# A mixture-of-experts layer on one core: weights in a ring of four thirds, TensorE's code written out per ring position, and list rows taken earlier on VectorE

## The chip, the core and the metric

The kernel runs on one core of a Trainium2 chip. Its engines are TensorE (PE in the rows; PEld is its weight load), VectorE (DVE), ScalarE (ACT), GpSimd (POOL) and SyncE (SP, which here issues the weight transfers). The metric is the device time of one execution in microseconds.

## What is computed

One layer on 1024 tokens of width 1024. A mixer comes first (a gated linear recurrence and a spatial gating unit between two projections, with adaptive norms); the part of this study is the mixture of experts behind it, 32 experts, four for each token:

```python
logits = hf @ router_w + router_b
top_logit, top_e = lax.top_k(logits, 4); gates = softmax(top_logit)
# for each block of rows of one expert e:
gu = xb @ w_gu[e] + b_gu[e]                 # 1024 -> 2048, f32
g, lin = split(gu); g = min(g, 7); lin = clip(lin, -7, 7)
ys = (g * sigmoid(1.702 * g) * (lin + 1)) @ w_down[e] + b_down[e]
out[row_tok] += ys * row_gate               # then residual, rmsnorm
```

All weights are f32: 8 MB of `w_gu` and 4 MB of `w_down` for each expert.

## The kernel before

The mixer and the router take the first 480 us or so. Then the tokens of each expert are cut into units of 32 rows, and up to four units form an item, which all engines handle in one pass of a loop. The router's result makes a table of items in SBUF (`items_i`): for each item its expert, first row, number of units, units before it, and its expert's place in the order. The places alternate between experts with many and with few tokens, and the last ones are alike. How many units an item has is read into registers at run time; `by_units` branches over the code for units that are not there. Here there are 32 places, 47 items and 143 units.

An expert's weights come in 12 chunks of 1 MB, numbered q, in three thirds of four: chunks 0 to 3 are the rows k 0 to 3 of the gate and linear weights, 4 to 7 the rows k 4 to 7, and 8 to 11 the down weights. They lie in `big`, six slots of 16 KB in each partition, and each third has its fixed two slots (`gu_slab`, `down_slab`, `chunk_tile`). SyncE's queue loads place after place. Before a third it waits until TensorE has released that third in the last item of the place before:

```python
if q % 4 == 0:
    sp_.wait_ge(freed[q // 4], done)
load_chunk(e, q)
```

`freed[0]` rises with the first matmul of the second half of the gate and linear product, `freed[1]` with the first matmul behind that half (a list's), `freed[2]` with the first matmul behind the down product. TensorE waits for each chunk with `w_arrived[q]` in the first unit of an item.

TensorE's loop, for item g: `down_of(g)` makes the list of item g+5 (`make_list`, L1159), multiplies the units by the down weights (L1226) and repeats the list's rows over partitions (`repeat_rows`, L1171); then `gate_and_linear_of(g + 1)` multiplies the next item's rows by the gate and linear weights (L1206), first half k 0 to 3 for all units, then the second. So the loop's back edge stands between a gate product and the down product of the same item.

VectorE's pass for item g: turn the gathered rows of item g+1 (`block_rows`, L1818), make the one-hot table of g+3 (L1810), the activations of g's units (L1858 to L1873), take the repeated list rows of g+4 and make indices and gates of g+2 (L1679 to L1695), read list g+5 (L1674), and write the results (L1878, L1881). GpSimd gathers the rows of g+2 when their indices are there, and then scatters the results of g into `acc_rows`. ScalarE scales the turned rows (`z_made`) and does the sigmoids.

The tile `r1` (32 KB in each partition) holds the hidden rows until they have been written out before the experts, and again at the end for the last norm.

## Time and profile before

| | |
|---|---|
| median of three executions | 2146.21 us (2138.85 to 4163.29) |
| the profiled execution | 2144.11 us, span 2142.4 us |
| mean granted TensorE clock | 0.968 |
| TensorE, VectorE, GpSimd, ScalarE busy | 91%, 47%, 24%, 17% |
| moved by DMA | 527 MB, 246 GB/s over the span |
| experts' part, first to last gate or down matmul | about 480 to 2111.6 us |

A row of the timeline merges equal instructions; in brackets stands the engine's idle time before them and who ended it. Busy shares of TensorE count its matmuls at whatever clock it had.

### The profile page before, as it was taken

Reading aid. Unit: us, or ns where it says so; the run is one execution under the profiler, and the core shown is the slowest. Engines: PE = TensorE matmul, PEld = TensorE weight load, DVE = VectorE, ACT = ScalarE, POOL = GpSimd, SP = SyncE. Lnnn points to the kernel's source line nnn. Section 1 sums busy time; section 2 is a strip of 40 time slices with the busy share of each in tenths; the row PEclk is TensorE's granted clock in tenths of the full one; section 3 lists DMA queues with packets and bytes.
Section 4 is the critical chain, followed back from the end, with each engine's and each line's share of the span. In section 5 each row is a group of like instructions: output and inputs, shape, how many; then the busy total and the mean of one; then the engine's idle time right before and its main releaser. Section 6 shows DMA issues by size and latency. Waiting matters only on the chain.

```text
span 2142.4 us, 53085 instructions
## 1 busy us (share of the span) xinstructions
PE 1960.0 (91%) x20253; PEld 803.5 (38%) x20254; DVE 1004.2 (47%) x2276; ACT 355.7 (17%) x729; POOL 508.6 (24%) x536
## 2 busy tenths in 40 slices
PE   3998999978989989999999998999999999999994
PEld 2443444432424323433343342334333343334332
DVE  6427756345434434444444454444443544444434
ACT  3025311221011111111111111111111111011012
POOL 3000022121312322313131322233233322322322
PEclk9998999988989989999999999999999999999997
DMA  9332126322581773959496969879797897999985
GB/s 330 128 118 78 63 95 196 138 109 97 197 340 29 237 300 95 353 177 355 161 352 224 355 251 367 301 266 391 256 387 252 296 357 266 386 385 338 325 305 187
DMA packets 128956, 527.19 MB, mean 246 GB/s; under 512 B 17184, under 2 KB 47920, under 8 KB 79760
## 3 DMA queue, kind: packets, MB, share of 16 engines
q1 hardware_dynamic: 95344, 470.39, 56.6%
q0 software_dynamic: 33568, 56.29, 11.4%
q8 instruction: 19, 0.31, 0.1%
q14 instruction: 25, 0.20, 0.0%
HBM read 494.22 MB, written 32.38 MB: 246 GB/s over the span
## 4 chain that ended last, share of the span: by engine, by line
PE 74%; DMA 14%; DVE 5%; SPq 3%; ACT 2%; issue 1%; POOL 1%; DVEq 0%; POOLq 0%; ACTq 0%
PE psum L1206 39%; PE psum L1226 21%; DMA big<-in_exp_w_down_dram 6%; DMA big<-in_exp_w_gu_dram 6%; PE psum L1115 5%; PE psum L959 5%; PE psum L1052 2%; SPq L466 1%; DMA big<-in_w_in_dram 1%; PE psum L999 1%; DVE big L1453 1%; SPq L447 0%; PE psum L1159 0%; DVE r L1926 0%; DVE gacc L1391 0%
## 5 line engine op out<-in xcount | busy, mean ns | idle before, releaser
L1206 PE MATMUL psum<-big,r 128*32 128x512 f32 x9152 | 1017.5, 602 | 53.8 <-DMA big<-in_exp_w_gu_dram 42.6
L1206 PEld LDWEIGHTS psum<-big,r 128*32 128x32 f32 x9152 | 290.3, 111 | 732.5 <-issue 653.8
L1226 PE MATMUL psum<-big,r 128*32 128x256 f32 x9152 | 518.3, 385 | 27.3 <-DMA big<-in_exp_w_down_dram 16.4
L1226 PEld LDWEIGHTS psum<-big,r 128*32 128x32 f32 x9152 | 294.1, 111 | 230.1 <-DMA big<-in_exp_w_down_dram 26.3
L859 ACT ACTIVATE r<-r,shift 128x128 f32<-128x128 f32 x376 | 154.2, 480 | 998.8 <-PE psum L1206 941.7
L666 POOL DMA_INDIRECT acc_rows<-r,scatter_idx x143 | 230.8, 1614 | 84.9 <-POOL scatter_idx L697 42.9
L655 POOL COPY gather_idx<-r 128x4 int32 (+1 forms) x48 | 8.9, 186 | 1017.5 <-DVE r L1688 1017.5
L1858 DVE TENSOR_TENSOR r<-psum,r 128x256 f32<-128x256 f32 x143 | 60.6, 424 | 377.7 <-PE psum L1206 376.8
L658 POOL DMA_INDIRECT r<-hs_rows,gather_idx x192 | 192.3, 1002 | 85.3 <-issue 45.4
L1818 DVE STREAM_TRANSPOSE r<-r 128x1024 f32<-128x1024 f32 x47 | 97.9, 2084 | 175.8 <-DMA r<-hs_rows,gather_idx 112.6
L959 PE MATMUL psum<-r,big 128*128 128x512 f32 x384 | 167.8, 598 | 2.8 <-DMA big<-in_w_in_dram 2.8
L1878 DVE TENSOR_TENSOR r<-psum,r 128x256 f32<-128x256 f32 x143 | 60.8, 425 | 227.8 <-PE psum L1226 214.0
L866 ACT ACTIVATE r<-r 128x256 f32<-128x256 f32 x143 | 59.5, 416 | 393.6 <-DVE r L1864 393.6
L1115 PE MATMUL psum<-big,r 128*128 128x512 f32 x256 | 112.2, 595 | 0.6 <-DMA big<-in_w_out_dram 0.4
L959 PEld LDWEIGHTS psum<-r,big 128*128 128x128 f32 x384 | 73.4, 192 | 94.1 <-issue 91.1
L1873 DVE STREAM_TRANSPOSE r<-r 128x256 f32<-128x256 f32 x143 | 93.5, 654 | 4.9
L1869 DVE TENSOR_TENSOR r<-r 128x256 f32<-128x256 f32 x143 | 60.8, 425 | 50.3 <-ACT r L866 50.3
L1881 DVE SCALAR_TENSOR_TENSOR r<-r,g1row,g_rows 128x256 f32<-128x256 f32 x143 | 69.3, 485 | 5.1
L1115 PEld LDWEIGHTS psum<-big,r 128*128 128x128 f32 x256 | 47.9, 190 | 59.0 <-issue 57.7
L1391 DVE SCALAR_TENSOR_TENSOR gacc<-big,cact,gacc 128x512 f32<-128x512 f32 x84 | 63.2, 752 | 3.0
L608 POOL TENSOR_TENSOR r<-r,big 128x512 f32<-128x512 f32 x8 | 12.0, 1496 | 216.6 <-DVE r L1545 216.6
L1871 DVE TENSOR_TENSOR r<-r 128x256 f32<-128x256 f32 x143 | 60.8, 425 | 4.9
(284 smaller groups left out, 975.1 us busy)
## 6 DMA issues: line engine op xcount, KB each, us to landing
big<-in_exp_w_gu_dram SPq DMA_DIRECT2D x256, 1024.0 KB, 10.5
big<-in_exp_w_down_dram SPq DMA_DIRECT2D x128, 1024.0 KB, 14.0
big<-in_ada_w_dram SPq DMA_DIRECT2D x12, 2048.0 KB, 12.8
r<-in_x_dram SPq DMA_DIRECT2D x16, 512.0 KB, 12.5
big<-in_w_in_dram SPq DMA_DIRECT2D x4, 2048.0 KB, 20.3
r<-in_exp_b_gu_dram SPq DMA_DIRECT2D x128, 64.0 KB
big<-in_w_out_dram SPq DMA_DIRECT2D x2, 2048.0 KB, 13.3
hs_rows<-r POOLq DMA_DIRECT2D x8, 512.0 KB, 2.9
```

The source lines that it names most:

```text
L658: pool.indirect_dma_start(z_quarters[:, u, :], None, hs_quarters, bass.IndirectOffsetOnAxis(ap=gather_idx[:, u:u + 1], axis=0)).then_inc(r ...
L666: pool.indirect_dma_start(acc_quarters, bass.IndirectOffsetOnAxis(ap=scatter_idx[:, u:u + 1], axis=0), y_sb[:, u, :], None, bounds_check=4 ...
L859: ins_ = act.activation(izT[:, k, :].rearrange("p (u n) -> p u n", u=UMAX), z_blocks[:, :, k, :], ACT.Identity, bias=shift2[:, 1, k:k + 1] ...
L959: last = pe.matmul(b, w[:, k, m * P:(m + 1) * P], zT[:, k, th * 512:(th + 1) * 512], start=(k == 0), stop=(k == KT - 1))
L1115: last = pe.matmul(b, src[:, ct % CT, t * P:(t + 1) * P], ring(("wout", dh))[:, ct, :], start=(ct == 0), stop=(ct == 2 * CT - 1))
L1206: last = pe.matmul(psum[32 * j:32 * j + 32, u, :].rearrange("p (a n) -> p a n", a=2), izT[:, k, u * UNIT:(u + 1) * UNIT], rhs[:, :, 256 * ...
L1226: ins_ = pe.matmul(psum[32 * i:32 * i + 32, 4 + u % 2, 0:256], actT[:, u, f, :], down_slab(f)[:, 256 * i:256 * i + 256], start=(f == 0), s ...
L1391: ins_ = dve.scalar_tensor_tensor(out=a, in0=w[:, k, :], scalar=cact[:, k:k + 1], in1=a, op0=ALU.mult, op1=ALU.add)
L1818: dve.transpose(z_blocks, z_quarters.rearrange("p u (n k) -> p u k n", k=KT)).then_inc(z_blocked, 1)
L1869: dve.tensor_tensor(gsig_sb[:, u % 2, :], gate_u, sig_sb[:, u % 2, :], ALU.mult).then_inc(gsig_made, 1)
L1873: dve.transpose(actT[:, u, :, :], act_sb[:, u % 2, :].rearrange("p (n k) -> p k n", k=KT)).then_inc(at_made, 1)
L1881: dve.scalar_tensor_tensor(out=y_sb[:, u, :], in0=y_sb[:, u, :], scalar=gate_cur[:, u:u + 1], in1=g2_rows[:, :], op0=ALU.mult, op1=ALU.mul ...
```

## The change

There are four thirds in the ring: the three in `big`, and `r1` as the fourth. Third c of place p lies in ring third (3p + c) mod 4, so the position of an expert's weights repeats every four places. A third is loaded when the third four loads before it has been released: that is the down third of place p-2 for c = 0, and the two gate thirds of place p-1 for c = 1 and 2. The semaphores of arrival exist twice, for even and odd places.

Since TensorE's addresses are fixed in its code, its body is written once for each of the four positions. Place 0 has its own code, places 1 to 28 go through an outer loop of seven trips over four bodies, and places 29 to 31 have three more. Each body is a loop over the items of its place, with ends read from the table. Within an item the gate and linear product now comes first and the down product second, which is the same sequence of products as before with the loop's edge elsewhere.

On VectorE, `rows_here`, `make_idx` and `make_gates` move from behind the activations to the place behind `block_rows`.

```diff
@@ SyncE and the tiles
-        w_arrived = [sem(f"w_arrived{q}") for q in range(CHUNKS)]
+        w_arrived = [[sem(f"w_arrived{q}_{turn}") for q in range(CHUNKS)] for turn in range(2)]
+        def third_of(place, c):
+            return (3 * place + c) % THIRDS
+        def in_third(third, at, size):
+            if third == THIRDS - 1:
+                return r1[:, at:at + size]
+            return big[:, SLOT_OF_PAIR[2 * third + at // 4096], at % 4096:at % 4096 + size]
-        def gu_slab(k):
-            at = (k % 2) * 2048
-            return big[:, SLOT_OF_PAIR[k // 2], at:at + 2048]
+        def gu_slab(place, k):
+            return in_third(third_of(place, k // 4), (k % 4) * 2048, 2048)
...
             for place in range(1, NE):
-                done = sp_.value_load(items_i[0:1, CUM_ITEMS + place - 1:CUM_ITEMS + place], min_val=1, max_val=MAX_ITEMS)
+                done_before, done = done, items_until(place - 1)
                 for q in range(CHUNKS):
-                    if q % 4 == 0:
-                        sp_.wait_ge(freed[q // 4], done)
-                    load_chunk(e, q)
+                    if q == 0 and place >= 2:
+                        sp_.wait_ge(freed[2], done_before)
+                    if q == 4:
+                        sp_.wait_ge(freed[0], done)
+                    if q == 8:
+                        sp_.wait_ge(freed[1], done)
+                    load_chunk(place, e, q)
@@ TensorE
             def begin_item():
-                pe.reg_alu(place, loaded[0], 0, ALU.max)
-                pe.reg_alu(units, loaded[1], 1, ALU.max)
-                pe.reg_alu(before_, loaded[2], 0, ALU.max)
-                pe.reg_mul(arrived, place, SEMW)
-                pe.reg_add(arrived, arrived, SEMW)
+                pe.reg_alu(units, loaded[0], 1, ALU.max)
+                pe.reg_alu(before_, loaded[1], 0, ALU.max)
+            def begin_place(at):
+                if at % 2 == 0:
+                    pe.reg_add(arrived, arrived, SEMW)
+                pe.reg_alu(first_item, next_item, 1, ALU.max)
+                pe.reg_alu(next_item, loaded[2], 1, ALU.max)
...
-            with pe.Fori(0, last_item) as g:
-                down_of(g)
-                begin_item()
-                gate_and_linear_of(g + 1)
-            down_of(last_item)
+            def items_of(at, start, place):
+                with pe.Fori(start, next_item) as g:
+                    begin_item()
+                    gate_and_linear_of(at, g, place)
+                    down_of(at, g)
+            down_of(0, 0)
+            by_units(pe, next_item, 1, lambda: items_of(0, 1, 0))
+            with pe.Fori(0, (NE - 4) // THIRDS) as i:
+                for at in range(1, THIRDS + 1):
+                    begin_place(at)
+                    items_of(at, first_item, i * THIRDS + at)
+            for place in range(NE - 3, NE):
+                begin_place(place)
+                items_of(place, first_item, place)
@@ VectorE
                 block_rows(g + 1)
+                rows_here(g + 4, step)
+                make_idx(g + 2, step)
+                make_gates(g + 2, step)
                 make_onehot(g + 3)
...
                 by_units(dve, units, 1, activate_1)
-                rows_here(g + 4, step)
-                make_idx(g + 2, step)
-                make_gates(g + 2, step)
                 read_list(g + 5)
```

TensorE, between the last down product of one item and the next gate product. Before (L1171 repeats the list's rows, L1188 sets the item's registers, L1206 is the first unit's gate product; no branch stands between them):

```order
L1171 MATMUL psum<-g1row,r2 128x6 x4
L1188 ISA
L1206 MATMUL psum<-big,r2 32x512 x16
L395 COMPARE_AND_BRANCH
L395 UNCONDITIONAL_BRANCH
```

Now, at the end of the first of the four bodies (L1249 is the down product, L1187 the repeat, L1380 the loop over a place's items, L1213 the next place's registers, L1229 the gate product of the next body):

```order
L1249 MATMUL psum<-big,r2 32x256 x32
L398 UNCONDITIONAL_BRANCH x3
L1187 MATMUL psum<-g1row,r2 128x6 x4
L1380 REGISTER_ALU
L1380 COMPARE_AND_BRANCH
L1213 ISA
L1380 UNCONDITIONAL_BRANCH
L1380 ISA
L1229 MATMUL psum<-big,r2 32x512 x16
L396 COMPARE_AND_BRANCH
L396 UNCONDITIONAL_BRANCH
```

The back edge has moved to this place, and a place's registers are set behind it. The outer loop holds four such bodies one behind the other, where the loop before held one.

SyncE's queue, the second third of a place (place 2 before, place 2 now), behind the bias rows of that place. Before:

```order
L473 ISA
L473 DMA r2<-in_exp_b_gu_dram 32x2x256
L476 ISA
L476 DMA r2<-in_exp_b_down_dram 32x256
L466 ISA [waits freed1]
L466 DMA big<-in_exp_w_gu_dram 128x2048
```

Now:

```order
L480 ISA
L480 DMA r2<-in_exp_b_gu_dram 32x2x256
L483 ISA
L483 DMA r2<-in_exp_b_down_dram 32x256
L473 ISA [waits freed0]
L473 DMA r1<-in_exp_w_gu_dram 128x2048
```

The wait is for the release of the first third instead of the second, and this load goes to `r1`.

VectorE, the head of the loop's pass, from the transpose of gathered rows on. Before, the one-hot table (L1800, L1810) follows it:

```order
L1818 STREAM_TRANSPOSE r<-r 128x1024 [waits z_made1,z_made0,rows_in]
L388 ISA
L388 TENSOR_LOAD r
L388 ISA x3
L388 TENSOR_LOAD r
L388 ISA x2
L1800 ISA
L1800 COPY g1row<-r 128x48
L1810 ISA
L1810 REGISTER_ALU
L1810 TENSOR_TENSOR r<-r 128x1024
```

Now the list rows and the indices stand there (L1720 to L1729), and the one-hot table behind them:

```order
L1859 STREAM_TRANSPOSE r<-r 128x1024 [waits z_made1,z_made0,rows_in]
L1719 REGISTER_ALU
L1720 COPY g1row<-psum 128x24 [waits rows_repeated]
L1886 ISA
L1725 SCALAR_TENSOR_TENSOR g1row<-g1row 128x4 [waits dve_chain]
L1886 REGISTER_ALU
L1727 SCALAR_TENSOR_TENSOR g1row<-g1row,slot_quarter 128x4 [waits dve_chain]
L1886 REGISTER_ALU
L1729 ISA [waits dve_chain]
L1729 SCALAR_TENSOR_TENSOR r<-g1row,quarter 128x4
L1735 TENSOR_TENSOR g1row<-g1row 128x4
```

Six small operations have moved ahead of the one-hot table, with a wait for the repeated rows in front of them.

## Rows read from the trace of the kernel before

**Rows 1.** The page's sections 1 and 2: busy share, and 40 slices of the span.
```profile
PE 1960.0 (91%) x20253; PEld 803.5 (38%) x20254; DVE 1004.2 (47%) x2276; ACT 355.7 (17%) x729; POOL 508.6 (24%) x536
...
GB/s 330 128 118 78 63 95 196 138 109 97 197 340 29 237 300 95 353 177 355 161 352 224 355 251 367 301 266 391 256 387 252 296 357 266 386 385 338 325 305 187
```

**Rows 2.** TensorE's waits from 546.5 us.
```profile
PE psum L1206 <- DMA big<-in_exp_w_gu_dram: 42.6, 25, 2.8
PE psum L1226 <- DMA big<-in_exp_w_down_dram: 16.4, 16, 1.5
PE psum L1226 <- DVE r L1873: 6.2, 2, 3.1
```

**Rows 3.** The chain of waits, 1827 to 1902 us: start us, us, what.
```profile
1827.87 20.74 PE psum L1206 x192
...
1859.58 27.60 PE psum L1206 x256
1887.18 0.29 PE psum L1159 x8
...
1901.60 0.55 PE psum L1206
```

**Rows 4.** Windows: us, busy us (x count) of PE, PEld, DVE, ACT, POOL; clock, DMA, GB/s.
```profile
546.50:588.50 42.00, 42.00 (x528) 16.85 (x525) 18.73 (x47) 4.86 (x12) 10.77 (x11) 1.00 0.68 235
605.80:2111.60 1505.80, 1444.80 (x17680) 565.48 (x17680) 673.45 (x1688) 196.02 (x486) 407.11 (x399) 0.98 0.78 285
1849.00:2111.00 262.00, 262.00 (x3332) 107.19 (x3328) 117.72 (x301) 31.07 (x77) 69.29 (x67) 1.00 0.87 318
...
40.00:480.00 440.00, 398.98 (x1310) 190.06 (x1310) 231.46 (x348) 116.43 (x145) 46.11 (x51) 0.96 0.35 123
```

**Rows 5.** SyncE's queue, 1566 to 1589 us: start us, us, issues merged.
```profile
1566.20 1.89 SPq L466 DMA_DIRECT2D big<-in_exp_w_gu_dram  x4
...
1575.76 1.92 SPq L466 DMA_DIRECT2D big<-in_exp_w_gu_dram  x4
1586.55 1.88 SPq L466 DMA_DIRECT2D big<-in_exp_w_down_dram  x4
```

**Rows 6.** DMA engines from 1626 to 1659 us: queue, packets, MB, share.
```profile
q1 hardware_dynamic: 2017, 11.41, 88.9%
```

**Rows 7.** TensorE's timeline, passes of one unit (751) and two (1586).
```profile
751.19 4.13 PE L1226 MATMUL psum<-big,r 128*32 128x256 f32 x48 [3.09 <-DVE r L1873]
...
1586.20 0.25 PE L1171 MATMUL psum<-g1row,r 128*128 128x6 bf16 x4
1586.38 9.65 PE L1206 MATMUL psum<-big,r 128*32 128x512 f32 x88
1596.57 4.50 PE L1206 MATMUL psum<-big,r 128*32 128x512 f32 x40 [0.54 <-DMA big<-in_exp_w_gu_dram]
```

**Rows 8.** VectorE by line, 606 to 2111 us; its timeline at 748 and 1671.
```profile
L1818 DVE STREAM_TRANSPOSE r<-r 128x1024 f32<-128x1024 f32 x44 | 91.7, 2084 | 168.1 <-DMA r<-hs_rows,gather_idx 112.6 <-issue 55.4
...
748.07 0.42 DVE L1858 TENSOR_TENSOR r<-psum,r 128x256 f32<-128x256 f32 x1 [0.86 <-PE psum L1206]
...
1670.47 0.13 DVE L1679 COPY g1row<-psum 128x24 f32<-128x24 f32 x1
...
1671.74 0.16 DVE L1695 TENSOR_TENSOR r<-g1row 128x4 f32 x1
```

**Rows 9.** DMA queues: 40 to 480, 500 to 606, and two in 606 to 2095.
```profile
q8 instruction: 11, 0.18, 0.2%
...
q8 instruction: 6, 0.10, 0.4%
...
q0 software_dynamic: 27295, 40.19, 12.9%
q14 instruction: 16, 0.13, 0.0%
```

**Rows 10.** The chain's last transfer but one.
```profile
2114.68 3.66 DMA acc_rows<-r,scatter_idx
```

100 lines of the change are left out of this document (55 added, 45 removed).

## The prediction

> **What bounds the kernel now.** I read the page's busy shares first: TensorE is busy 91% of the span [rows 1], and no other engine reaches 50%. The experts' part therefore hangs on TensorE, and the question is what it loses there. The waits of TensorE from 546.5 us on have only three entries: 42.6 us for chunks of the gate and linear weights, 16.4 us for chunks of the down weights, 6.2 us in two waits for VectorE's turned activations [rows 2]. Nothing else holds it.
>
> Then the price of an undisturbed pass. With no wait a pass of four units takes 27.60 us for gate and linear, 0.29 for a list and 14.13 for the down product and the rows' repeat, 42.0 in all, and one of three units 31.7 (from 1827.87 to 1859.58) [rows 3]; so a unit costs 10.4 us (6.9 gate and linear, 3.5 down) and a pass 0.45 on top. Counting the matmuls of each pass in the timeline, the stretch from 605.8 us to the last matmul at 2111.6 has 44 passes: 15 of four units, 17 of three, 11 of two and one of one unit. Undisturbed that is 15 x 42.0 + 17 x 31.7 + 11 x 21.4 + 11.0 = 1415 us. (That is 134 units: at 128 matmuls a unit and 12 a pass they make the 17,680 of the window's row, [rows 4].) It took 1505.8 us, so 90.5 us are lost: 61.0 idle (it was busy 1444.8), and 29.5 in which TensorE ran, but partly at the lower of its clock's two levels: the stretch has a mean granted clock of 0.98, the undisturbed end from 1849 on 1.00 and no idle time [rows 4]. Of the 90.5, 6.5 belong to the pass of one unit near 751 us, whose down product waits for its own activations [rows 7]: no weight is late there. **84 us hang on late weights**, waits and the slower clock behind them.
>
> Why they are late: the queue that loads weights waits until the third of the ring that it refills is released, and the release is in the same expert's last pass. In rows 5 the loads of one expert go out at 1566.20, 1575.76 and 1586.55 us, the moments at which the previous expert (its pass began 31.7 us before 1586.38, at 1554.7, [rows 7]) lets go of its thirds. Over the stretch behind them the DMA engines are nearly full: the weights' queue has 88.9% of their time and brings 11.41 MB in 33 us [rows 6]. So a chunk of 1.05 MB takes 3.0 us as it stands, 2.7 if the queue had all their time, and an expert's twelve 32 to 36 us, but a pass of three units lasts 31.7 and one of two 21.4. So after short passes TensorE meets chunks that have not landed: 0.54 us and then more in the pass that begins at 1586.38 [rows 7], 59.0 us in all.
>
> **The ring of four thirds.** Third c of place p now replaces the third used four loads earlier: its first third waits for the down product of place p-2, its second for the first half of p-1, its last for the second half of p-1. Everything may start one third earlier, 10 to 15 us. For the expert of rows 5: its first third could go at 1554.8 instead of 1566.2, the second at 1566.2 instead of 1575.8, the last at 1575.8; behind each other at 2.9 us a chunk they end near 1567, 1579 and 1591, and the down product wants the last only at 1601 [rows 5, 7]. The stall is gone with 8 us to spare.
> I stepped through all passes in this way (units from the instruction counts, four chunks per third, each 2.85 to 2.95 us and 2.3 us more until landing, no load before its third is released). With the releases of before it gives 57 to 78 us of waits where the trace has 59.0 [rows 2], and at the same passes; with the releases of the change 3 to 7 us, nearly all in two passes that follow very short experts. With the lower clock behind them I leave 7 us: **84 - 7 = 77 us gained**. Place 1 loads its first third already when the item table is ready, near 500 us, into the tile that held the hidden rows; the DMA engines are nearly idle there (the slices near 500 us have 97 and 197 GB/s, [rows 1]), so I take nothing for it.
>
> **VectorE's order.** The list rows of item g+4 and the indices of g+2 are made ahead of the activations instead of behind them. Its transpose of gathered rows waited 112.6 us for gathers [rows 8], but TensorE has no wait for gathered rows in this stretch [rows 2], so the earlier gather gains nothing on the path. What moves ahead is six small operations, from 1670.47 to 1671.90: 1.5 us. What is queued behind them is the one-hot table and the first activation, for which TensorE waits in turn. Even in the pass of one unit VectorE sat idle 0.86 us before that activation, until the gate product was there [rows 8]; a unit more gives 6.9 us more. So only two passes, of one unit each, lose 0.6 us: **1 us lost**.
>
> **TensorE's program.** Before, one body served all passes. A pass of four units executes 256 + 256 + 12 matmuls (256 and 8 of them in [rows 3]) and as many weight loads, with some 40 register and branch instructions about 1,090. Now four such bodies stand in a row inside the outer loop, three more behind it. What code costs to bring in shows only before: eleven code packets of 16 KB (0.18 MB) on queue 8 fall between 40 and 480 us, in which 1,310 matmuls and 1,310 loads ran, so with the waits between them a packet holds about 256 instructions and a body is 4.2 of them; and from 606 to 2095 us queue 8 has none [rows 4, 9]. So a body once fetched stays, across 45 back edges. And while the first trip brought its body in, with six packets between 500 and 606 us, the gate product from 546.5 ran at full speed: 42.0 us busy of 42.0 [rows 4, 9]. Straight code is therefore hidden. Four bodies are 17 packets; the trace shows at least five held at once, and does not show seventeen. If those do not stay, the inner loops (14 back edges in places with several items) still find their own body, but the outer loop's back edge, taken six times, finds its first block gone, and nothing can be fetched ahead of a jump back by 17 blocks. The price of one such miss no row has. From below it is nothing; from above I take the nearest transfers that nothing overlaps, above all the last scatter's 3.66 us [rows 10], with as much again for a second block and the slower clock: 0 to 8 us. TensorE's queue covers little, since the matmuls of the down product leave it fastest. I take 3.5 us, near that row: **6 x 3.5 = 21 us lost** (0 to 48).
> The rows say that code of 4.2 blocks is kept through 45 jumps back. The Trainium skill, "Runtime: NRT & Kernel Launch", section "Instruction fetch mechanics", has both sides: TensorE's instruction memory is 128 KiB, eight blocks of 16, which this agrees with; and a taken branch whose target is outside a window of two pages stalls for a fetch, which it does not, since each back edge of before goes back four blocks and no packet follows. By the eight blocks the sum stays as it is.
> The new words on a place (one compare, a few register operations and a load more) stand where the last down product is still queued; the boundary of before has no idle time between the repeat and the next product (1586.20 + 0.25, then 1586.38, [rows 7]), and I take zero, 0.3 us x 31 = 9 at most.
>
> **Sum**, against the profiled execution's own 2144.1 us (span 2142.4 and 1.7 around it; 2.1 below the median of the runs shown, 2146.2): 2144.1 - 77 + 1 + 21 = 2089, so **2090 us**, 2.6% below.
>
> **Rivals.** *Code is also missed at forward jumps.* A pass with fewer than four units jumps over up to three branches of its body, and counted along the built program with the units of each pass, 37 such jumps in first visits cross a block's end. No row of before shows a jump into code not yet fetched (its first trip had all four units), so this can be. If the block after the target is then late, 2.2 us each time: 37 x 2.2 = 81 us on top, 2171 us, slower than before; it turns slower than before from 1.5 us a jump. Against it: a block ahead was always there in the first trip. The skill's window of two pages, on the page named above, would also act here and at the 14 inner back edges.
> *Nothing is missed*: the outer loop's code stays or is fetched behind the queue. 2144.1 - 77 + 1 = 2068.
> *The thirds come no sooner in effect*: loads that start earlier meet the scatter and gather packets (12.9% of the DMA engines' time [rows 9]) and the chunks take 3.3 us; then the walk leaves some 20 us of waits and 12 of slow clock, 25 more than I took, with the code's part 2115; were only half the waits to go, 2128.
>
> **How the numbers follow.** The forecast has 0.55 (2072 to 2112), nothing missed 0.15 (2068), the jumps 0.18 (2120 to 2195), late chunks 0.12 (2110 to 2135). The range 2063 to 2140 leaves out most of the jumps' case. A measurement of this kernel tells about 2% from no change: faster means below 2103, slower above 2189. Faster: nearly all of the first two, 0.67; same 0.26; slower 0.07, from the jumps' case with 3 us and more each.
>
> **What would show it.** Waits of TensorE for the weights' DMA under 10 us in all, a mean clock of 1.00 from 800 us on, the weights' queue waiting on the repeat of the list rows. Code packets on queue 8 going on through the experts' part, some 130; a gap of TensorE with no releaser at every fourth place (six of them), and none in passes with a jump. VectorE's wait for gathers well under 112 us. I am wrong if those gaps come at every place, if they are longer than 8 us, or if the weights' waits stay above 30 us.

## The result and the profile after

The changed kernel takes 2195.2 us (median of four, 2191.7 to 2197.1), the kernel before in the same comparison 2144.4: a ratio of 1.024, 95% interval 1.022 to 1.027. Two later comparisons gave 1.023 and 1.022. It is slower by 51 us where 2.6% faster was forecast; 2195 lies outside the range.

The profiled execution took 2196.3 us, span 2194.6, 52 more than before. TensorE's waits from 546.5 us (us in total, times, longest), which answer to [rows 2]:

```profile
PE psum L1229 <- issue: 39.6, 25, 6.3
PE psum L1187 <- issue: 38.9, 15, 5.4
PE psum L1249 <- issue: 8.8, 7, 1.6
PE psum L1175 <- DVE r L1851: 5.9, 2, 2.9
PE psum L1249 <- DVE r L1917: 5.3, 2, 2.6
```

The weights have left the list altogether: not one wait for a chunk is left of 59.0 us. In their place stand 47 waits "<- issue", 87.3 us, idle time for which the profile shows no releaser, at the gate product (L1229), the repeat (L1187) and the down product (L1249). The windows that answer to [rows 4] (us, busy us (x count) of PE, PEld, DVE, ACT, POOL, then clock, DMA share, GB/s):

```profile
546.50:588.50 42.00, 42.00 (x532) 16.84 (x528) 18.93 (x48) 4.85 (x12) 11.87 (x11) 1.00 0.62 221
605.80:2163.80 1558.00, 1464.77 (x17724) 596.37 (x17720) 683.03 (x1690) 196.09 (x486) 433.65 (x398) 0.97 0.78 275
1901.00:2163.80 262.80, 261.64 (x3324) 108.53 (x3317) 117.73 (x294) 31.08 (x77) 70.70 (x62) 1.00 0.83 292
615.20:2163.80 1548.60, 1460.83 (x17664) 594.55 (x17668) 680.18 (x1688) 196.09 (x486) 432.01 (x397) 0.97 0.78 275
```

From 605.8 us to the last matmul the experts' stretch is 1558.0 us instead of 1505.8. The changed kernel is already 9.4 us behind at its start: it has the rest of a pass of one unit in there, with a gap of 5.0 us behind it. The 44 passes of before begin only at 615.2 (last row) and take 1548.6 us, 42.8 more: idle is 87.8 instead of 61.0, and the other 16 us are matmuls at the lower clock (1460.8 busy instead of 1444.8). The last passes, of four units each, are undisturbed as before. The page's DMA queues:

```profile
q1 hardware_dynamic: 95344, 470.39, 56.1%
q0 software_dynamic: 33568, 56.29, 11.6%
q8 instruction: 163, 2.67, 0.5%
q14 instruction: 25, 0.20, 0.0%
```

Queue 8, which carries code, alone from 606 to 2095 us, where before it moved nothing [rows 9]:

```profile
q8 instruction: 135, 2.21, 0.6%
```

So the code packets are there that the prediction gave as "some 130". Where the gaps are shows in TensorE's timeline: first a pass of one unit, which answers to the first of [rows 7], then the outer loop's back edge and the pass of two units behind it, and one of the later back edges (start us, us; in brackets the idle time before):

```profile
744.17 7.07 PE L1229 MATMUL psum<-big,r 128*32 128x512 f32 x64
754.18 0.37 PE L1175 MATMUL psum<-g1row,r 128*128 128x6 bf16 x8 [2.93 <-DVE r L1851]
757.19 5.51 PE L1249 MATMUL psum<-r 128*32 128x256 f32 x64 [2.64 <-DVE r L1917]
767.52 0.24 PE L1187 MATMUL psum<-g1row,r 128*128 128x6 bf16 x4 [4.82 <-issue]
768.24 10.25 PE L1229 MATMUL psum<-big,r 128*32 128x512 f32 x80 [0.47 <-issue]
...
874.96 0.25 PE L1187 MATMUL psum<-g1row,r 128*128 128x6 bf16 x4
877.88 2.77 PE L1229 MATMUL psum<-r 128*32 128x512 f32 x21 [2.66 <-issue]
883.36 6.61 PE L1229 MATMUL psum<-r 128*32 128x512 f32 x42 [2.71 <-issue]
...
897.48 7.11 PE L1249 MATMUL psum<-big,r 128*32 128x256 f32 x128
908.89 0.25 PE L1187 MATMUL psum<-g1row,r 128*128 128x6 bf16 x4 [4.30 <-issue]
...
1502.62 13.86 PE L1229 MATMUL psum<-r 128*32 128x512 f32 x95 [6.32 <-issue]
```

These gaps end with code. From 546.5 us on 25 gaps without a releaser are longer than 0.8 us, and each of them ends 2.4 to 3.0 us after a packet of queue 8 begins (worked out from the packets' start times).

There are two kinds of gap. One stands at each of the six outer back edges (877.88, 1110.14, 1316.31, 1502.62, 1690.87, 1876.09), ahead of the first body's gate product: 33.3 us idle in all, 3.9 to 6.3 each. Behind the one at 1502.62 the granted clock is 0.79, and 95 matmuls take 13.9 us that elsewhere take 10.3. The other, 54 us, stands mostly behind short down products on a first visit to a body: in front of the repeat at 767.52 and 908.89. First visits of four units have at most 0.5 us ahead of their gate product, and the same holds for a place's second item in the same body.

Per pass, from one gate product's start to the next (mean us of two profiles of each kernel; a first visit is a place's first item; worked out from the matmuls' start times, without place 0; the undisturbed pass of one unit is an estimate from the others, 10.3 us a unit):

```
units  visit  passes  undisturbed  before  changed
1      first     2        11.1      17.3    23.9
2      first    11        21.4      25.7    27.0
3      first     9        31.7      34.2    33.9
3      later     8        31.7      31.7    34.9
4      first     9        42.0      43.8    42.6
4      later     6        42.0      42.0    43.0
```

The later visits of three and four units that grow are those in front of an outer back edge. Of the eleven first visits of two units three stand behind one and take 32 to 34 us; the other eight average 24.9 (22.3 to 27.0). On VectorE the transpose no longer waits for gathers (before 112.6 us, [rows 8]):

```profile
L1859 DVE STREAM_TRANSPOSE r<-r 128x1024 f32<-128x1024 f32 x47 | 97.0, 2064 | 116.3 <-issue 111.2 <-DMA r<-hs_rows,gather_idx 5.1
```

### The profile page after: what moved, and what is told of

Same layout as the page of the kernel before. It is cut to its first block, busy times and chain, and to the rows that moved or that the text cites. A ratio compares the mean times of both kernels' runs of the same rounds, so it can differ in the third digit from the quotient of the medians.

```text
span 2194.6 us, 53308 instructions
## 1 busy us (share of the span) xinstructions
PE 1976.3 (90%) x20253; PEld 833.1 (38%) x20254; DVE 1013.7 (46%) x2276; ACT 356.0 (16%) x729; POOL 535.3 (24%) x536
## 4 chain that ended last, share of the span: by engine, by line
PE 83%; issue 5%; DVE 5%; DMA 2%; ACT 2%; SPq 1%; DVEq 1%; POOL 1%; ACTq 0%; POOLq 0%
PE psum L1229 46%; PE psum L1249 23%; PE psum L1131 5%; PE psum L975 4%; PE psum L1068 2%; DMA big<-in_w_in_dram 1%; PE psum L1015 1%; PE psum L1175 1%; DVE big L1494 1%; SPq L454 0%; DVE r L1967 0%; SPq L463 0%; DVE gacc L1432 0%; PE psum L1187 0%; DVE big L1510 0%
## 5 line engine op out<-in xcount | busy, mean ns | idle before, releaser
L1229 PE MATMUL psum<-big,r 128*32 128x512 f32 x6912 | 780.5, 606 | 17.7 <-issue 9.8
L1249 PE MATMUL psum<-big,r 128*32 128x256 f32 x7744 | 431.1, 381 | 12.4 <-issue 5.9
L1229 PEld LDWEIGHTS psum<-big,r 128*32 128x32 f32 x6912 | 238.6, 112 | 516.0 <-issue 506.3
L1249 PEld LDWEIGHTS psum<-big,r 128*32 128x32 f32 x7744 | 248.6, 110 | 177.2 <-issue 11.0
L1229 PE MATMUL psum<-r 128*32 128x512 f32 x2240 | 265.0, 618 | 33.3 <-issue 33.3
L674 POOL DMA_INDIRECT r<-hs_rows,gather_idx x192 | 222.9, 1161 | 87.8 <-issue 45.7
L1229 PEld LDWEIGHTS psum<-r 128*32 128x32 f32 x2240 | 81.3, 113 | 205.5 <-issue 205.4
L1249 PE MATMUL psum<-r 128*32 128x256 f32 x1408 | 80.9, 386 | 5.5 <-issue 2.9
L1913 DVE TENSOR_TENSOR r<-r 128x256 f32<-128x256 f32 x143 | 60.9, 426 | 50.1 <-ACT r L882 50.1
## 6 DMA issues: line engine op xcount, KB each, us to landing
big<-in_exp_w_gu_dram SPq DMA_DIRECT2D x192, 1024.0 KB, 10.6
```

The source lines that it names most:

```text
L674: pool.indirect_dma_start(z_quarters[:, u, :], None, hs_quarters, bass.IndirectOffsetOnAxis(ap=gather_idx[:, u:u + 1], axis=0)).then_inc(r ...
L1229: last = pe.matmul(psum[32 * j:32 * j + 32, u, :].rearrange("p (a n) -> p a n", a=2), izT[:, k, u * UNIT:(u + 1) * UNIT], rhs[:, :, 256 * ...
L1249: ins_ = pe.matmul(psum[32 * i:32 * i + 32, 4 + u % 2, 0:256], actT[:, u, f, :], down_slab(at, f)[:, 256 * i:256 * i + 256], start=(f == 0 ...
L1913: dve.tensor_tensor(gsig_sb[:, u % 2, :], gate_u, sig_sb[:, u % 2, :], ALU.mult).then_inc(gsig_made, 1)
```

## The experiments

Theory A, formed from this trace: TensorE's code arrives one block of 256 instructions at a time, the next is asked for only when the one before is entered, and comes about 5.9 us later; a body has 4.2 blocks whatever its units, so a first visit lasts some 25 us, and at an outer back edge nothing is there at all. Rival B is the one on record, a price of some 2.2 us for each jump over a block's end. Others: VectorE's move, and the ring itself (the tile `r1`, more DMA at a time). In two of the five comparisons that follow the kernel before took 2218 us (beside VectorE's move, the bodies alone, the loop written out and three jumped blocks) and 2193 us (beside the repeated move and the two forms with two bodies), in the others 2143 to 2146. The end of this section comes back to that; the kernels of those two are read by their own medians and traces. Each of the five ran on a chip of its own, so differences between kernels of different comparisons rest on their times being the same on those chips: the change took 2191.5 and 2191.9 us on two of them, and VectorE's move alone 2158.1 and 2158.5 on the two others.

**VectorE's move alone.**

```diff
                 block_rows(g + 1)
+                rows_here(g + 4, step)
+                make_idx(g + 2, step)
+                make_gates(g + 2, step)
                 make_onehot(g + 3)
...
-                rows_here(g + 4, step)
-                make_idx(g + 2, step)
-                make_gates(g + 2, step)
```

> The kernel before with VectorE's move alone (list rows, indices and gates ahead of the one-hot table and the activations). Three theories of the 51 us by which the change lost. Theory A (TensorE's code arrives too slowly for short passes and is missed at the outer back edge) and theory B (code missed at each jump over a block's end) both put nothing here: 2144 to 2150 us, with 1.5 us more in front of the one-hot table of a pass of one unit and VectorE's wait for gathers down from 112 us to under 20. Theory C, the move delays what TensorE waits for: 2165 us and more.

2158.1 us; span 2157.7. Against the kernel before of its own comparison that is a ratio of 0.973, against the medians of before elsewhere, 2144, it is 14 us more, between what theories A and B gave (2144 to 2150) and what C gave (2165 and more). The waits of TensorE from 546.5 us:

```profile
PE psum L1206 <- DMA big<-in_exp_w_gu_dram: 41.7, 28, 2.9
PE psum L1226 <- DMA big<-in_exp_w_down_dram: 17.8, 16, 2.0
PE psum L1159 <- DVE r L1810: 5.9, 2, 3.0
PE psum L1226 <- DVE r L1876: 5.3, 2, 2.7
```

The weights' waits are those of before (59.5 us), and in the two passes of one unit the one-hot table is now late as well. It was repeated later:

> The kernel before with VectorE's move alone, once more: in its first comparison the kernel before took 2218 us on that chip, which no profile explains, and on two others 2144. If the move costs what the two profiles show (2157.7 against 2142.4 and 2142.9 us), the ratio is 1.007 (2155 to 2162); if that chip alone made it so, 1.000 to 1.002.

2158.5 us, span 2156.9; the kernel before 2192.7 this time, ratio 0.984 (0.982 to 0.986). The move alone costs some 14 us against a kernel before of 2144, and not 1. Five of them are seen as waits; the rest lies in passes of three and four units that follow short ones and in the clock, and I haven't traced it further.

**The change without it**: the same three lines put back.

> The changed kernel with VectorE's order as before; all else stays. With the move alone the profiled span was 2157.7 us against 2142.4 and 2142.9 of two profiles of the kernel before, of which the two passes of one unit explain 3 us, where I had forecast 1 us in all. If the move costs the same inside the change, this gives 2175 to 2180 us; if it only costs where nothing else is late, 2187 to 2192.

2187.9 us, ratio 1.019 (1.017 to 1.021) against 1.022 and 1.023 of the whole change. Inside the change the move costs about 4 us by the medians of the same level (2191.5 and 2191.9) and 6 to 8 by those two ratios, whose intervals overlap with this one. So it is a small part of the loss of 46 to 51 us, some 4 to 8 us of it.

**The four bodies with a ring of three.**

```diff
         def third_of(place, c):
-            return (3 * place + c) % THIRDS
+            return c
...
-                    if q == 0 and place >= 2:
-                        sp_.wait_ge(freed[2], done_before)
-                    if q == 4:
-                        sp_.wait_ge(freed[0], done)
-                    if q == 8:
-                        sp_.wait_ge(freed[1], done)
+                    if q % 4 == 0:
+                        sp_.wait_ge(freed[q // 4], done)
```

> The changed kernel's TensorE program (four bodies in the outer loop, item loops, parity semaphores) and VectorE order, but all bodies read the same three thirds, and the loads wait for their releases as before: the ring of four is taken out. Theories A and B: the code's idle time stays (about 80 us of gaps without releaser) and the waits for weights come back, less than the 59 us of before because short passes are now longer: 2215 to 2265 us. Theory C, the ring itself or its releases cost the time (more DMA contention, the tile that held the hidden rows): back to 2144 to 2155.

2209.5 us, just under the range. Its waits:

```profile
PE psum L1225 <- issue: 39.7, 23, 5.8
PE psum L1183 <- issue: 32.3, 10, 6.2
PE psum L1225 <- DMA big<-in_exp_w_gu_dram: 16.9, 13, 2.1
...
PE psum L1245 <- issue: 5.4, 4, 2.7
PE psum L1245 <- DMA big<-in_exp_w_down_dram: 5.3, 5, 1.4
```

77 us without a releaser, with the old addresses and releases: the gaps come with the four bodies and not with the ring. Of the 59 us of waits for weights only 22.2 return, since the passes that were too short for their weights are now longer than they. What the ring of four saves this program is therefore only 14 to 18 us (2209.5 less 2195.2 to 2191.5, across comparisons). This is where most of the expected gain went: late weights and late code hit the same short passes.

**The outer loop written out**: `for place in range(1, NE)` instead of the outer loop and its three places behind.

> The changed kernel with its outer loop written out: 31 bodies in a straight line, no outer back edge. Theory A: the six gaps at an outer back edge (33 us idle, 5.5 each, and the slower clock behind them) go, the gaps in passes of one, two and three units stay: 2150 to 2162 us, every pass of one or two units on its first visit at 24 to 26 us. Theory B (a price per jump): the same total, but the gaps move with the jumps' places relative to the blocks' ends. If instead the loop's code of 17 blocks was partly kept and used again on later trips, written out it is worse: above 2200.

2158.4 us, 33 to 37 less than the changed kernel in its three comparisons, and 61.3 us "<- issue" instead of 87.3:

```profile
PE psum L1187 <- issue: 39.6, 11, 5.7
PE psum L1229 <- issue: 12.3, 15, 3.5
PE psum L1249 <- issue: 7.8, 7, 2.0
```

The waits of the gate product, where the back edges were, have shrunk; those in front of the repeat (L1187), behind short passes, stay: first visits of two units take 26.8 us on average, as in the change (27.0). So an outer back edge costs 6 us net. At its own place it costs more, some 9 us (the pass in front of it is longer by 3 to 7 us than with the loop written out, the one behind by 2 to 5), and the other passes together are some 15 us shorter; why is not shown.

**One more block in each body, jumped over.** It tells A from B.

```diff
+            def hop(blocks):
...
+                with pe.If_lt(units, UMAX + 1):
+                    pe.nop()
+                with pe.Else():
+                    for _ in range(128 * blocks):
+                        pe.matmul(psum[:, 6, 0:6], onehot[:, 0, :], cur6[:, 0, :], start=True, stop=True,
+                                  skip_group_check=True)
...
                     gate_and_linear_of(at, g, place)
+                    hop(1)
                     down_of(at, g)
```

> The changed kernel with one more block of code in each body, never executed, jumped over between the gate product and the down product. Theory A (blocks come in order, one at a time, about 5.9 us apart, whatever is jumped over): a first visit now lasts at least 5.3 x 5.9 = 31 us, so passes of one and two units grow by 6 to 7 us, those of three by 0 to 2, those of four not at all: 14 short first visits, about 2280 us. Theory B (a price of about 2.2 us for each jump over a block's end): all 31 first visits grow by 2.2 us, those of four units as well: 2260 us. Theory A2 (only the block behind the running one is fetched ahead, so a jump over a whole block finds nothing): a full miss of 5.5 us in each of 31 first visits, 2360 us.

2281.2 us, ratio 1.064 (1.062 to 1.066): 90 us more than the change. Its two largest waits from 546.5 us, and in the timeline two first visits, of three and of two units:

```profile
PE psum L1175 <- issue: 97.5, 26, 7.5
PE psum L1229 <- issue: 38.1, 20, 6.0
```

```profile
1644.57 20.81 PE L1229 MATMUL psum<-big,r 128*32 128x512 f32 x192
1667.73 0.35 PE L1175 MATMUL psum<-g1row,r 128*128 128x6 bf16 x8 [2.35 <-issue]
...
1681.07 14.92 PE L1229 MATMUL psum<-big,r 128*32 128x512 f32 x128
1699.41 0.37 PE L1175 MATMUL psum<-g1row,r 128*128 128x6 bf16 x8 [3.42 <-issue]
```

The mean first visit grew, against the second profile of the change, by 4.9 us with one unit, 4.5 with two, 2.9 with three and 0.2 with four; later visits not at all. Rival B, a price per jump, would give the same to all; a full miss for each jumped block would give 5.5 to all. Neither holds: a jumped block costs only as much as the work in front of it fails to cover. At four units a gate product lasts 27.7 us, and on average nothing is left of it, though single passes of the nine change by 1.9 us down to 2.2 up. That is theory A. Its total, 2280, came out only because two misses met: the short passes grew by 4.5 to 4.9 us instead of 6 to 7, and those of three units by 2.9 instead of 0 to 2, since 5.3 blocks take about as long as their 31.7 us.

How long a block takes isn't a fixed figure. In the change the packets around a pass of two units begin at 875.06, 880.98, 886.90, 893.32, 899.52, 906.19 and 912.32, so 5.9 to 6.7 us apart, with a DMA share of 0.99. In an undisturbed first visit of four units they are up to 14 us apart (1963.31, 1976.83, 1988.43, 1994.76), so the fetch follows the work and doesn't run ahead of it; that it is the entry into a block that asks for the next is inferred from this. Where the engines are nearly idle they can come closer together: the last pass of the kernel with the down third doubled, below, has them at 2055.42, 2059.46 and 2063.37 (DMA share 0.24), with TensorE waiting for the first two. Some come 3 to 4 us apart under a full load as well. No run changed the load alone, so whether the weights' traffic makes code late stays open.

**How much code stays.** Four kernels with the loop of before and more code in it: three and five blocks never executed and jumped over (`hop(3)`, `hop(5)` between the down product and `begin_item`), the whole body written twice and taken in turn, and the same with the second half of the gate product shared.

```diff
+            def by_turn(body):
...
+                with pe.If_lt(turn_, 1):
+                    body()
+                with pe.Else():
+                    body()
...
             with pe.Fori(0, last_item) as g:
-                down_of(g)
-                begin_item()
-                gate_and_linear_of(g + 1)
+
+                def pass_():
+                    down_of(g)
+                    begin_item()
+                    gate_and_linear_of(g + 1)
+
+                by_turn(pass_)
+                pe.reg_alu(turn_, turn_, 1, ALU.bitwise_xor)
```

> The kernel before with three blocks' worth of code (384 matmuls with their loads) that is never executed, jumped over once in each pass between the down product and the next gate product: the body is 7.3 blocks instead of 4.3. If TensorE keeps eight blocks and a jump within kept code is free: 2144 to 2150 us and no code packets in the experts' part after the first trips. If it keeps only about the five blocks that the trace of before shows, each pass finds its first block gone: at least 5.5 us a pass, 2390 us and more.

> The kernel before with five blocks of code that is never executed, jumped over once in each pass: a loop of 9.3 blocks. The loops of 6.3 and 7.3 blocks had no code packet after the first trips. If the limit is the place for eight blocks, counted over all that lies between the first and the last, each pass now fetches its code again: a miss of 5.5 to 6.3 us at the back edge, one more at the hop, and no pass shorter than its blocks arrive; with the five blocks that are executed alone each pass lasts at least 37 us, about 2650 us in all; if the hopped blocks are fetched too, 55 us a pass and 3150 us. If only executed blocks are kept and counted: 2144 to 2225, like the loop of 7.3.

> The kernel before with the body of its item loop written twice (the same weights, the same waits), the passes taking one and the other in turn: 8.6 blocks of code, all of them executed, where the padded loops of 7.3 and 9.3 had 4.3 executed ones. If TensorE keeps eight executed blocks, nothing is kept here: each of 46 passes begins with a jump over or back by more than four blocks, 5.5 us idle and the slower clock behind, and passes of two units last at least 25 us: 2400 to 2460 us, with some 200 code packets. If more is kept (16 would do, and then the 17 blocks of the change just miss it): 2144 to 2155.

> As the loop of two bodies, but with the second half of the gate and linear product shared: 7.5 blocks, all executed. If eight are kept: 2145 to 2155 us, a few code packets more in the first trips and none behind. If the limit is nearer the 6.3 executed blocks that the kernel with two down products kept: as the loop of two bodies, 2350 us and more.

With three jumped blocks 2222.3 us at a kernel before of 2218.2 (ratio 1.002), with five 2147.6 at 2145.7 (1.001, interval 1.000 to 1.002): both cost nothing, and both have 21 code packets in all, where before has 19. The two bodies took 2349.6 and the shared form 2298.4 at a kernel before of 2192.7 (1.071 and 1.048), the first less than the 2400 to 2460 that I expected, the second between its two forecasts. Their code packets from 606 to 2050 us:

```profile
q8 instruction: 212, 3.47, 1.0%
```

```profile
q8 instruction: 149, 2.44, 0.7%
```

Counted by me in the built programs (no trace shows where a block ends), the code in use in a pass or in two touches 6 blocks with the jumped ones (out of 8 and 10 that the loop spans), and 9 and 8 with the two bodies; the kernel with two down products, below, uses 7 and keeps them. So up to 7 blocks in use stay, 8 do not, and blocks that are only jumped over don't count. By size alone, 6.3 blocks in use stay and 7.5 do not. My expectation for 7.5 blocks was wrong: it took blocks by their size and not by the ends they cross. The Trainium skill, "Runtime: NRT & Kernel Launch", section "Instruction fetch mechanics", gives TensorE 128 KiB of instruction memory, refilled in blocks of 16 KiB, so eight blocks. The runs keep at most seven; that the eighth is taken by the block fetched ahead would fit, but none of them shows it. The outer loop of the change, with 17, is far above.

**Better without code: weights released by chunk.** The ring stays three thirds and the body one; only the release changes.

```diff
+                    if k < KT - 1:
+                        last.then_inc(chunk_read[k], 1)
...
                 for q in range(CHUNKS):
-                    if q % 4 == 0:
-                        sp_.wait_ge(freed[q // 4], done)
+                    sp_.wait_ge({KT - 1: gu_made, CHUNKS - 1: dn_made}.get(q, chunk_read[q]), read)
                     load_chunk(e, q)
```

(`read` is the number of units in the places before, from the same table; in the down product `chunk_read[8]` to `[10]` rise in the same way.)

> The kernel before with one body and three thirds, but each weight chunk released by itself: the last matmul that reads chunk q in each unit counts up a semaphore of its own, and the weights' queue waits for as many units as the places before have. The same walk through the passes that gave the forecast has 62 us of waits for weights with releases by thirds (the trace of before has 59) and 30 with releases by chunk. No code is added to TensorE, so theory A expects no gap without releaser: 84 us of cost fall to about 42, 2102 us (2085 to 2120). If the DMA engines are the bound rather than the late release, waits and time stay: 2135 to 2144.

2106.9 us, ratio 0.982 (0.979 to 0.985). The waits for weights fell to 32.3 us, and no wait is without a releaser:

```profile
PE psum L1206 <- DMA big<-in_exp_w_gu_dram: 23.6, 17, 2.5
PE psum L1228 <- DMA big<-in_exp_w_down_dram: 8.7, 8, 1.4
PE psum L1228 <- DVE r L1877: 6.2, 2, 3.1
```

**And with the down weights' third alone doubled** into `r1`, so that only the down product exists twice in the one body:

```diff
+                with pe.If_lt(odd_place, 1):
+                    down_by(0)
+                with pe.Else():
+                    down_by(1)
```

> The kernel before with releases by chunk and with the down product's third alone doubled (odd places read it from the tile that held the hidden rows), so that TensorE's one body has two down products, 6.3 blocks in all instead of 18 in the loop. The walk has 21 us of waits: 84 us fall to about 30, 2090 us (2075 to 2110), if a body of 6.3 blocks stays and runs at full speed. If it behaves as the padded body of 7.3 blocks did (3.2 us in each pass of three and four units), 70 to 100 us are added: 2160 to 2190. If a larger body is fetched again at each back edge, at least 5.5 us in each of 46 passes: 2340 and more.

2109.3 us, ratio 0.983 (0.980 to 0.987): no better than by chunk alone, and at the upper end of the range. The waits for down weights are gone, but the last pass, which stands behind the loop, is new code with a jump over two blocks in it:

```profile
2056.02 0.35 PE L1177 MATMUL psum<-g1row,r 128*128 128x6 bf16 x8
2058.17 1.24 PE L1252 MATMUL psum<-r 128*32 128x256 f32 x17 [1.79 <-issue]
2061.74 15.37 PE L1252 MATMUL psum<-r 128*32 128x256 f32 x239 [2.34 <-issue]
```

The last place is an odd one, so its branch can be dropped (`if last: down_by((NE - 1) % 2)`):

> The kernel with releases by chunk and the down product's third doubled, but the down product of the last item, which stands behind the loop, written for odd places alone (the last place is 31). The trace of that kernel had 6.8 us more in this pass than the kernel before: code that was jumped to two blocks ahead. If those are missed code, 2109 falls to 2103 (2100 to 2105); if they are not, it stays.

2102.6 us, ratio 0.980 (0.978 to 0.982), as forecast (the walk's 2090 for the doubled third stays unreached: it had 21 us of waits for weights, and 25.7 are left); in the trace the same product now follows at once:

```profile
2055.84 0.35 PE L1177 MATMUL psum<-g1row,r 128*128 128x6 bf16 x8
2056.13 14.02 PE L1252 MATMUL psum<-r 128*32 128x256 f32 x256
```

This is the best kernel of the study, 43 us below the kernel before and some 90 below the change. Most of the gain is the release by chunk; what the doubled third adds to it, 0.982 to 0.980, lies within the intervals.

**The kernel before at three speeds.** Controls, unchanged, to find why it took 2218 and 2193 us in two comparisons:

> The kernel before, unchanged, with a profile of its own: in the last comparison its unprofiled runs took 2218 us, against 2144 in the comparison with the change, while the kernel with VectorE's move alone, which has the same TensorE program, took 2158. If the kernel has two levels of speed that do not hang on the source (74 us apart), this run shows either about 2144 us with the pass table of the trace of before, or about 2218 us with something in each pass of three and four units, as the padded body has it (3.2 us behind the third unit's down product, no weights late). If the 2218 was only a slower chip, all stretches are longer alike. The ratio to before is then 1.00 on the same chip.

> The changed kernel, unchanged, beside the kernel before on one more chip. Theory A (its code arrives too late) puts the same 80 us of gaps without releaser and 2190 to 2200 us. If the changed kernel has levels of its own, the time moves by tens of us and the gaps lie in other passes.

> The kernel before, unchanged, to get a trace of it where it is slow, if this chip is such a one. Theory G: on some chips POOL's four indirect gathers, issued 5.3 to 10.2 us after a down product starts, starve TensorE of instructions from about the 145th matmul of that product on, in each pass of three or four units, 2.2 to 3.3 us each: 33 such passes behind the first, 50 to 75 us. The trace then shows idle time of the weight loads (no releaser) beside POOL's gathers and down products of 12.9 to 14 us instead of 10.7 for three units, at about 2192 to 2218 us in all. On a chip where it does not happen: 2143 us as twice before. The ratio to before is 1.00 either way.

> The changed kernel, unchanged. It takes the list rows at the top of VectorE's pass, so that its gathers do not lie beside the down product. Theory G: it takes 2190 to 2197 us on any chip, and where the kernel before is at 2192 or 2218 its ratio is 1.00 or 0.99 instead of 1.02. If the slow chips are slow for another reason, it is slower there too and the ratio stays 1.02.

> The best kernel so far (releases by chunk, the down product's third doubled, the last down product for odd places alone), which has VectorE's order of before and so its gathers beside the down product. Where the kernel before is at 2143: 2103 us, ratio 0.980. Where it is at 2192 to 2218, theory G puts the same 50 to 75 us on this one: 2150 to 2180, ratio again about 0.98.

They fell in comparisons where it took 2143.5 and 2146.1: itself 2144.1 and 2145.7 (1.000 both), the change 2191.5 and 2191.9 (1.023 and 1.022), the best kernel 2102.1 (0.980, interval 0.978 to 0.982). So the verdicts stand, but the slow level was not caught with a trace of that kernel. What the traces of the two slow comparisons do show: the kernels with VectorE's order of before (three jumped blocks, the two forms with two bodies) have 18 to 22 us in which the down product waits without a releaser, mostly in its third unit, so in passes of three and four units. In the kernel with three jumped blocks, which has no code packet there (PEld is TensorE's weight load):

```profile
1697.32 0.99 POOL L658 DMA_INDIRECT r<-hs_rows,gather_idx  x1 [0.30 <-issue]
1698.61 0.95 POOL L658 DMA_INDIRECT r<-hs_rows,gather_idx  x1 [0.30 <-issue]
1698.84 0.17 PEld L1226 LDWEIGHTS psum<-big,r 128*32 128x32 f32 x5 [0.20 <-issue]
1699.59 0.17 PEld L1226 LDWEIGHTS psum<-big,r 128*32 128x32 f32 x6 [0.58 <-issue]
1699.86 0.95 POOL L658 DMA_INDIRECT r<-hs_rows,gather_idx  x1 [0.30 <-issue]
```

Its down products of three units take 13.8 us instead of 10.6, those of four 16.9 instead of 14.0; with the two bodies they take 13.2 to 13.3 and 16.4. The gaps begin some 8 us into the product, with GpSimd's third gather: in all 33 passes of three and four units the first long one ends 0.2 to 1.6 us behind that gather's start, whether it stands near the 140th weight load of the product or near the 180th. The kernels that gather earlier (VectorE's move alone, and the two with four bodies) had none of it in the same comparison. Over the 17 passes of three and 15 of four units that is 97 and some 82 us; less the 29 us of waits for weights that it covers (30.2 with three jumped blocks instead of 59.0) 68 and 53, near the 74 and 49 by which the kernel before was slower there. That the gathers are the cause is argued and not shown, and they can't be the whole of it: the trace of the kernel before has them at the same moments (5.3, 6.6, 7.9 and 9.3 us into the product) and no such gap. Whether the chip or the occasion makes it so can't be told either; it stays open. No comparison with the change fell at such a time. Its four bodies with a ring of three, 2209.5 us, had a ratio of 0.997 there, so the change itself, 14 to 18 us faster than they, might come out at 0.99 (an estimate from these times): the loss of 2% is shown where the kernel before takes 2144 us. Nor were the kernels with release by chunk run where it takes longer.

## Why the prediction was wrong

- *What bounds the kernel, and the 84 us on late weights*: right. With the four thirds all 59.0 us of waits for weights are gone; the walk through the passes had left 3 to 7 us of them. The same walk gave 30 us by chunk (measured 32.3) and 21 for the doubled down third (26.2 and 25.7).
- *77 us gained*: this failed as a term of a sum. It holds only while the passes are as short as before. Once a first visit lasts 24 us and more for its code, most weights would have come in time anyway: with the four bodies the ring of four is worth 14 to 18 us.
- *VectorE's order, 1 us*: too small; 14 us alone, about 4 inside the change. The waits that I named (the one-hot table in the passes of one unit) are 5 of them. A short pass has three places where it can be late, and I counted one.
- *"Straight code is therefore hidden"*: the step that failed. It rested on the first trip, which ran at full speed while its packets came in. That trip has four units, 42 us for 4.2 blocks, 10 us for each. I read it as "a block is always ahead" and not as a rate, and six packets in 106 us [rows 9] say nothing on passes of 11 and 21 us. A pass of two units has 5 us for each block of its body, whether it executes it or hops over it, and a block took 5.9. In the 42 us of that row itself only two packets fall (549.61 and 565.85). By this account late code in first visits is some 95 of the 131 us that the code costs (2195 less 2060, which is 2144 less the weights' 84, and less VectorE's 4); the outer back edges are the rest.
- *Six outer back edges at 3.5 us*: the right six places, and 135 code packets where I had 130, but 6 us each by the loop written out, 33 to 37 us in all instead of 21. The gap alone is 5.5 us on average; the nearest DMA transfer, 3.66 us, was too short a stand-in, with too little for the clock behind it.
- *A body once fetched stays over the inner back edges*: right.
- *Register words on a place: 0*: nothing of them is seen, at most the 0.5 us that stand on L1229 behind the gaps.
- *Rivals*: the jumps' rival (0.18) had the right kind of event, the right sign and the wrong mechanism. Its price per jump, 2.2 us, at 37 jumps gave 2171; a price per jump is ruled out by the block that was jumped over. That rival should have been worked out for a rate, pass by pass: with a first visit of 24 to 25 us that is some 3 us in passes of two units and 13 in those of one, and none in those of four.
- *What would show it*: weights' waits under 10 us, and the packets, came true, and VectorE's wait for gathers fell to 5.1 us. The queue's waits for the list rows' repeat (259.5 us, 29 times) say little, since the kernel before has them as well (240.8, 27 times). The clock did not reach 1.00 from 800 us, and gaps came "in passes with a jump", which I had excluded.

## What to carry to other kernels

Code is a stream with a rate: before a loop body is written several times, divide the time of its shortest pass by the blocks that it spans, hopped ones too (here a block took 5.9 us and more beside a full load of weights), and keep all code in use between two visits within seven blocks. Before buffers are added, look at how finely they are released: here a semaphore for each chunk gained 37 us without a byte of memory or another body, where an extra third, with the four bodies that it needs, lost 51. Two delays that hit the same short passes don't add, so neither do the gains of removing them.

## What the runs showed of the hardware

- A block of 256 TensorE instructions that is not kept comes about 5.9 us after the one before it while the DMA engines are nearly full (share 0.99), and TensorE goes on 2.4 to 3.0 us after its packet begins: a first visit of one unit takes 23.9 us for 4.2 blocks, 5.7 for each, though it jumps over most of them. Seven packets fell between 874 and 913 us, around a pass of two units:

```profile
q8 instruction: 7, 0.11, 1.1%
```

- With the DMA engines nearly idle (share 0.24) two such packets came 4.0 and 3.9 us after the one before; what part the load has in it is open.
- A jump back by 17 blocks left TensorE idle for 3.9 to 6.3 us; behind one of them, of 6.3 us, the granted clock was 0.79 for 13.9 us.
- Loops that use up to 7 blocks had no code packet behind the first trips; one that uses 8 had 149, one that uses 9 had 212.
- Blocks that a loop jumps over cost nothing if the rest stays: a loop that spans ten blocks and uses six ran as one of five.
- Indirect gathers of GpSimd beside a down product went along, in the traces of two of five comparisons, with a TensorE short of instructions that were kept; open, as told above.
